# A two-layer hybrid block on one core: K's copies under V's products, the gate's steps spread over the attention, three waits for all engines taken out

## What is computed

```python
h = rmsnorm(x, norm_mix_pre)
q, k, v, rw, gate_a, gate_b = split(h @ w_in)
y_att = sliding_window_attention(rope(q), rope(k), v, sinks) @ w_o_att   # 16 heads, 4 KV heads, window 128
y_rw = rwkv7_time_mix(rw, ...) @ w_o_rw                                  # 16 heads of 64, recurrence over time
mixed = sigmoid(gate_a) * y_att + sigmoid(gate_b) * y_rw
x = x + rmsnorm(mixed @ w_out, norm_mix_post)
```

## Time and profile before

| | |
|---|---|
| time, median of 3 runs (lowest, highest) | 4639.51 us (4636.82, 4644.62) |
| the profiled execution's own time | 4639.49 us |
| its span | 4638.0 us |
| mean granted clock of TensorE | 0.964 |
| busy: TensorE, its weight loads, VectorE, ScalarE, GpSimd | 93%, 73%, 43%, 33%, 12% |
| chain of work that ended last: TensorE | 52% of the span |
| attention of the first layer, first scores to the first column of the output projection | 125.5 to 234.7 us |
| its recurrence (scan), start and end | 489.2 to 664 us |

### The profile page before, as it was taken

The page is one execution under the profiler, slowest core; times in us unless marked ns, Lnnn a source line. Parts: engine busy times, 40 slices in busy tenths (PEclk is TensorE's granted clock), DMA queues, the critical chain, the costliest instruction groups (busy, mean ns, idle before and its releaser), DMA issues.

```text
span 4638.0 us, 76648 instructions
## 1 busy us (share of the span) xinstructions
PE 4333.9 (93%) x33564; PEld 3399.0 (73%) x33564; DVE 1980.6 (43%) x2957; ACT 1528.6 (33%) x2699; POOL 571.7 (12%) x398
## 2 busy tenths in 40 slices
PE   7899999899998899899899998988899999899999
PEld 5676896677776676896677776765778888666877
DVE  4536434455434536434455434347432221443332
ACT  2533232333332533232333333237321121343221
POOL 1215100011002215101011001102000000150000
PEclk9999999999998999999999998999999999899999
DMA  4122101244422122101344421110011111101222
GB/s 147 42 96 72 35 4 60 96 150 167 155 82 101 42 100 73 35 4 60 105 150 164 156 85 41 51 37 1 32 51 64 63 60 60 54 10 55 96 88 90
DMA packets 97647, 351.90 MB, mean 76 GB/s; under 512 B 10017, under 2 KB 13601, under 8 KB 95905
## 3 DMA queue, kind: packets, MB, share of 16 engines
q1 hardware_dynamic: 86432, 313.02, 19.7%
q10 hardware_dynamic: 10880, 33.96, 2.0%
HBM read 332.26 MB, written 14.68 MB: 75 GB/s over the span
## 4 chain that ended last, share of the span: by engine, by line
PE 52%; DVE 4%; ACT 1%; POOL 1%; issue 1%; ACTq 0%; DVEq 0%
PE ps L341 13%; PE ps L342 13%; PE ps L344 13%; PE ps L1260 5%; PE ps L2233 1%; DVE sml L2308 1%; POOL e L2753 1%; PE ps L2668 1%; PE ps L2670 1%; DVE hm_lo L428 1%; PE ps L2669 1%; DVE hm L437 1%; PE ps L2255 1%; PE ps L2536 1%; PE ps L2122 1%
## 5 line engine op out<-in xcount | busy, mean ns | idle before, releaser
L302 DVE TENSOR_TENSOR wlo<-ring,whi 128x1024 fp32r<-128x1024 f32 x494 | 626.2, 1268 | 1911.4 <-ACT whi L292 1911.2
L292 ACT CAST whi<-ring 128x1024 fp32r<-128x1024 f32 x494 | 517.8, 1048 | 2210.8 <-PE ps L344 1916.6
L341 PE MATMUL ps<-h_hi,whi 128*128 128x512 f32 x1424 | 597.6, 420 | 33.1 <-DVE wlo L302 16.5
L342 PE MATMUL ps<-h_lo,whi 128*128 128x512 f32 x1424 | 568.9, 400 | 0.0
L344 PE MATMUL ps<-h_hi,wlo 128*128 128x512 f32 x1424 | 568.1, 399 | 0.0
L341 PE MATMUL ps<-hm_hi,whi 128*128 128x512 f32 (+1 forms) x1408 | 518.6, 368 | 21.3 <-DVE hm_lo L428 21.3
L342 PE MATMUL ps<-hm_lo,whi 128*128 128x512 f32 (+1 forms) x1408 | 483.3, 358 | 0.0
L344 PE MATMUL ps<-hm_hi,wlo 128*128 128x512 f32 (+1 forms) x1408 | 421.3, 357 | 0.0
L341 PEld LDWEIGHTS ps<-h_hi,whi 128*128 128x128 f32 x1424 | 272.6, 191 | 178.8 <-issue 73.0
L341 PEld LDWEIGHTS ps<-hm_hi,whi 128*128 128x128 f32 x1408 | 268.2, 190 | 98.0 <-issue 19.9
L341 PE MATMUL ps<-ac_hi,whi 128*128 128x512 f32 x880 | 330.8, 376 | 6.4 <-DVE ac L2448 6.4
(11 more groups left out here) (394 smaller groups left out, 7610.5 us busy)
## 6 DMA issues: line engine op xcount, KB each, us to landing
ring<-in_w SPq DMA_DIRECT2D x590, 512.0 KB, 3.4
h_spill<-h ACTq DMA_DIRECT2D x2, 2048.0 KB, 6.7
x_spill<-x ACTq DMA_DIRECT2D x2, 2048.0 KB, 14.9
m_spill<-m ACTq DMA_DIRECT2D x2, 2048.0 KB, 9.4
h_again<-h_spill ACTq DMA_DIRECT2D x2, 2048.0 KB, 8.0
ma<-m_spill ACTq DMA_DIRECT2D x2, 2048.0 KB, 10.0
x<-x_spill ACTq DMA_DIRECT2D x2, 2048.0 KB, 10.1
x<-in_x SPq DMA_DIRECT2D x1, 2048.0 KB, 10.8
```

Of the source, the lines that this page charges most:

```text
L292: self.A.copy(self.hi[k % 2][:], raw).then_inc(self.s_cut_hi.h, 1)
L302: self.V.tensor_tensor(self.lo[k % 2][:], raw, self.hi[k % 2][:].bitcast(F32), ALU.subtract).then_inc(self.s_cut_lo.h, 1)
L341: T.matmul(ps[:, b, 0:cw], hi, xh(q, c0, cw), start=q == 0, stop=False, skip_group_check=True)
L342: T.matmul(ps[:, b, 0:cw], hi, xl(q, c0, cw), start=False, stop=False, skip_group_check=True)
```

## The change

Five things change, in both layers of the first block:

1. K's copies: `double(0)` runs before V's first look-ahead cut on ScalarE, `double(1)` after it; V's copy comes before the second cut.
2. The gate's 64 steps are dealt out by a table, `share`: none in round 0, then 4, 6, 3 in each of 14 rounds, 6, 6. `done(it)` gives the columns that end in round `it`. On ScalarE the copy of such a column stands right behind the round's exponentials, and its cuts at the round's end; on VectorE the cuts come before `att_lo`.
3. At the fence after the attention TensorE doesn't wait for the others; it waits for the last tile of `m`.
4. Both fences between the operands and the scan are gone. TensorE waits before each group's first product (`ready(g)`) for what that group reads. The scan's tiles that lie over the operands' last buffers get rooms of their own, and VectorE clears `st` when the last column is done.
5. `recurrence_operands` no longer cuts beyond its own pieces (`hold`). The two cuts left over and the transfer of `h_again` come in the scan, at the thirteenth place of ScalarE's and VectorE's woven programs.

```diff
     def fence(self, T_waits=True):
...
-        self.T.wait_ge(self.s_fence.h, end)
+        if T_waits:
+            self.T.wait_ge(self.s_fence.h, end)
...
-        self.fence()
+        T.wait_ge(self.s_gy.h, self.s_gy.n)
+        self.fence(T_waits=False)
...
-        self.recurrence_operands(hh, hl)
-        self.fence()
-        A.dma_start(self.view("h_again", TMP + 6144, DT, S)[:], self.h_spill.ap()).then_inc(self.s_ld_h.h, 16)
-        self.s_ld_h.take(16)
-        self.recurrence()
+        self.recurrence(*self.recurrence_operands(hh, hl))
...
         def act():
-            for st in rows:
-                if st.at + st.n == PIECE:
-                    self.act_cuts(self.ahead(st.cut))
-            A.wait_ge(self.s_roped.h, b_roped + n_out)
-            for g in range(4):
...
+            ends = [st for st in rows if st.at + st.n == PIECE]
+            double(0)
+            self.act_cuts(self.ahead(ends[0].cut))
+            double(1)
             A.wait_ge(self.s_mm.h, rows[-1].value)
             A.copy(vt[:], ps[:, 0:4, 0:256]).then_inc(self.s_vt.h, 1)
+            self.act_cuts(self.ahead(ends[1].cut))
...
+        share = [0, 4, 6, *[3] * (N - 2), 6, 6]
+        upto = [sum(share[:it + 1]) for it in range(N + 3)]
+
+        def done(it):
+
+            return range((upto[it] - share[it]) // DT, upto[it] // DT)
...
+        def pe_gate(it):
+            for i in range(upto[it] - share[it], upto[it]):
+                j, q = divmod(i, DT)
+                if q == 0 and j >= 1:
+                    T.wait_ge(self.s_gate.h, b_gate + j)
...
                     A.activation(es, es, ACT.Exp).then_inc(self.s_ex.h, 1)
+                act_gate(it)
...
-                    act_gate(j)
+                for j in done(it):
+                    self.act_cuts(self.ahead(cols[j][-1].cut))
...
+        def ready(g):
+
+            T.wait_ge(self.s_pc.h, b_pc + GP * (g + 1))
+            T.wait_ge(self.s_shift.h, b_sh + shifted((2, GP * (g + 1) - 1)) + 1)
+            T.wait_ge(self.s_zb.h, b_zb + N)
+            T.wait_ge(self.s_knn.h, b_knn + DT)
+            if g == 1:
+                T.wait_ge(self.s_bonv.h, b_bonv + DT)
+        return ready, cols[-1][-1].value
...
+        self.V.wait_ge(self.s_mm.h, columns_done)
         self.V.memset(m["st"][:], 0.0)
-        self.fence()
...
+        go(self.and_then(self.woven(lambda g: self.scan_act(g, m, ops, base[g])), 12, self.act_ahead))
+        go(self.and_then(self.woven(lambda g: self.scan_dve(g, m, base[g])), 12, lambda: self.dve_cuts(self.held)))
```

More of the change, by code:

```diff
@@ L534, in act @@
                     if st.at + st.n == PIECE:
-                        self.act_cuts(self.ahead(st.cut))
+                        self.act_cuts(self.ahead(st.cut) if hold is None else min(hold, self.ahead(st.cut)))
                 if act_tick:
@@ L544, in dve @@
                     if st.at + st.n == PIECE:
-                        self.dve_cuts(self.ahead(st.cut))
+                        self.dve_cuts(self.ahead(st.cut) if hold is None else min(hold, self.ahead(st.cut)))
                 if dve_tick:
@@ L817, in pe_values @@
             m.then_inc(self.s_pv.h, 1)
[L819 to L825, removed]
+        def pe_gate(it):
[3 more added lines that the diff above has]
+                    T.wait_ge(self.s_gate.h, b_gate + j)
+                hi, lo = self.halves_of(cols[j][q])
                 T.matmul(ps[:, 7, :], hi, hh(q, 0, S), start=q == 0, stop=False, skip_group_check=True)
@@ L844, in pe, with act_gate @@
             yield
[L846 to L848 removed]
+        def act_gate(it):
+            for j in done(it):
                 A.wait_ge(self.s_mm.h, cols[j][-1].value)
                 A.copy(GA[:, j, :], ps[:, 7, :]).then_inc(self.s_gate.h, 1)
[L851 to L856, removed]
         def dve_low(g):
@@ L933, in dve @@
                     V.tensor_copy(PT[j % 2][:, 0:2, 0:kw], heads(2)[:, :, 0:kw]).then_inc(self.s_ptv.h, 1)
[L934 to L937, removed]
+                for j in done(it):
+                    self.dve_cuts(self.ahead(cols[j][-1].cut))
+                if it >= 3 and steps[it - 3][0] == 3:
+                    dve_low(steps[it - 3][1])
             yield
@@ L1187, in free @@
                 T.wait_ge(self.s_zb.h, b_zb + n - 2)
-        go(*self.dense(cols, hh, hl, SEG1, lambda n: [n % 3], free, None, pe_tick, act_tick, dve_tick, pool_tick))
+        self.held = cols[-1][-1].cut + 2
+        go(*self.dense(cols, hh, hl, SEG1, lambda n: [n % 3], free, None, pe_tick, act_tick, dve_tick, pool_tick,
+                       hold=cols[-1][-1].cut))
         for n in range(N, max(at_bonus) + 1):
@@ L1225, in recurrence, with act_ahead, and_then @@
         base = [(pe[g], act[g], dve[g], pool[g]) for g in range(2)]
-        go(self.woven(lambda g: self.scan_pe(g, m, ops, base[g])))
-        go(self.woven(lambda g: self.scan_act(g, m, ops, base[g])))
-        go(self.woven(lambda g: self.scan_dve(g, m, base[g])))
+        go(self.woven(lambda g: self.scan_pe(g, m, ops, base[g], ready)))
+        go(self.and_then(self.woven(lambda g: self.scan_act(g, m, ops, base[g])), 12, self.act_ahead))
+        go(self.and_then(self.woven(lambda g: self.scan_dve(g, m, base[g])), 12, lambda: self.dve_cuts(self.held)))
         go(self.woven(lambda g: self.scan_pool(g, m, base[g])))
+    def act_ahead(self):
+        A = self.A
+        A.dma_start(self.view("h_again", TMP + 6144, DT, S)[:], self.h_spill.ap()).then_inc(self.s_ld_h.h, 16)
+        self.s_ld_h.take(16)
+        self.act_cuts(self.held)
+    def and_then(self, program, at, f):
+        for i, _ in enumerate(program):
+            if i == at:
+                f()
+            yield
     def woven(self, program):
@@ L1278, in scan_pe @@
         sp = self.s_sp[g].h
+        ready(g)
         for c in range(NCH + 1):
```

31 lines of the change are left out of this document (17 added, 14 removed).

## The result

| | before | after |
|---|---|---|
| time, median (lowest, highest) | 4641.5 us (4636.8, 4645.3), 6 runs | 4659.5 us (4655.8, 4661.4), 6 runs |
| ratio to before, 95% interval | | 1.0036 (1.0025 to 1.0048) |
| span of the profiled execution | 4638.0 us | 4657.0 us |
| mean granted clock | 0.964 | 0.966 |

The change is slower by 17 us (12 to 22). The forecast was +25, so the change in time was forecast 8 too high; the time itself lies 5 us under the forecast time, since the median of the kernel before is 2 us higher over all runs than over the three that the forecast started from.

The account below looks back on a forecast made before the run. TensorE, busy 93% of the span, was taken as the bound. Per layer, attention +13.3 and operands-to-scan -0.8, doubled, gave +25.0 on 4639.5: 4664.5 us; own range 4655 to 4675, 8-in-10 range 4643 to 4683.

Parts of the forecast that it names:

- V's and K's copies: Before the attention's first scores: K's copies run under V's products, only V's copy stays exposed, 6.2 us earlier per layer.
- The waits: Attention, per layer: TensorE's waits, mostly for the gate's copy, sum to 30.1 us against 11.4 before.
- VectorE enters round 6 some 1.8 late: Attention, rounds 7 and 15: round 4's cut delays VectorE 1.8 us, raising the wait from 7.4 to 9.2, twice.
- The clock: Attention, per layer: slow products after five long waits, 1.6 us each, cost 8.0 us, against 7.2 lost before.
- The attention as a whole: Per layer: new waits and clock loss, less the old ones and the 6.2 us from earlier copies, +13.3 us.
- The fence after the attention: End of attention: TensorE leaves once the last gated tile is written, but the fence passes right behind it: 0, at most -0.2.
- Operands to recurrence: Between operands and scan: the scan's first mask can start earlier without the fences and look-ahead subtraction, -3.3 us per layer.
- The held cuts: In the scan: two casts and a subtraction hold VectorE before the second group's `pf`, +2.5 us per layer, bounds 0 and 4.3.
- B: Rival: waits come as worked out, but cost no clock and the held cuts are hidden; 4643.5 us, chance 0.12.
- C: Rival: the gate's copy is in time after all, attention waits stay near those before; 4625.5 us, chance 0.08.
- D: Rival: the scan starts warm, its early product fills the wait and its start runs at full clock; 4642.9 us, chance 0.08.
- E: Rival: long attention waits cost 5.1 us of clock each, 17 in place of 8 in sum; 4682.5 us, chance 0.14.

Follow-up runs that it names:

- the fastest kernel above: Changed kernel with the gate's copy ahead of the round's exponentials on ScalarE and VectorE's low parts done one round later: 4600.4 us, 0.9916.
- Copy first: Changed kernel with one line moved: on ScalarE the gate column's copy stands ahead of the round's exponentials, not behind them: 4615.9 us, 0.9946.
- the last experiment: Copy first kernel with the last two weight cuts done among the operand columns again, not held for the scan; fences stay away: 4622.4 us, 0.9957.

## Why the prediction was right, and where its terms were off

**Direction and mechanism: right; that the time came so near is in part luck.** The loss is the gate's copy behind the exponentials of its own round: 33 us by the table, about 42 back by moving this one copy. But the sum said +12.5 per layer, 25.0 in all, and the layers gave 7.6 and 7.0, 14.6 in all. The other 4.4 of the 19.0 between the two profiled executions lie outside what was changed. With the layers' 14.6 alone the time would have been 4654.1, just under the forecast's own range of 4655 to 4675.

**V's and K's copies, -6.2: right.** First scores -5.3, and 0.9 of lateness before them makes -6.2. Alone they gave -11.6 for two layers.

**The waits, 30.1: 28.6 measured.** Round by round, forecast and trace: round 2 3.2 and 4.6; round 7 9.2 and 7.4; round 10 4.4 and 4.9; round 12 2.7 and 2.8; round 15 9.2 and 7.4; round 17 0.8 and 0.7. In round 12 the cause is the one I gave, VectorE's cut and `att_lo` in a row, but the last to be ready was ScalarE's `pt` and not the weighed `p`. Of rounds 7 and 15 the step that failed is "VectorE enters round 6 some 1.8 late": the mask of round 6 starts 0.6 behind the end of its scores (154.13 against 153.53), and TensorE comes 0.5 later to its wait than the 6.4 I gave it. The 1.8 was taken from a round before the change, one with the cut directly behind it; now the cut of round 4 is two rounds back. For round 2 I had taken 0.6 off for slow scores and let the third exponentials start 9.8 after the first scores; they start 10.5 after them.

**The clock, +0.8 over before: +0.5.** The difference was right and both sides were too high. The attention's products take 91.9 at 1.00 (the fastest kernel above), 97.8 before, 98.4 after: the low level cost 5.9 and 6.5 us where I had 7.2 and 8.0. (Copy first, also at 1.00, takes 93.0 for the same products; by that they are 4.8 and 5.4.) In the changed kernel the low level follows four waits and not the five I counted: 133.4 to 138.0 ran at 0.63, 167.8 to 171.5 at 0.50, 188.8 to 192.5 at 0.57 and 226.5 to 230.3 at 0.60, while the 6 us behind the wait of 2.8 ran at 1.00. Worked out from their busy times, an estimate, these four lost about 1.6 each, which is the price I had used. The Trainium skill (TensorE: Matmul & The Clock Gate, Terms) puts the penalty at half of the throttled time; as an estimate that is 0.08 x 126.9 = 10.2 for the changed kernel. The windows do not agree: about a third of that fell into TensorE's own waits.

**The attention as a whole, +13.3: +11.5** (17.2 more idle, 0.5 more busy, less 6.2).

**The fence after the attention, 0: right.** The wait is 3.1 as in the earlier trace rows, now put down to `m`.

**Operands to recurrence, -3.3: about -4.1 to -4.6.** Bonus product to mask is 1.15 now (497.95 to 499.10) against 3.63 in the earlier trace rows; 1.0 is the shorter tail: GpSimd's product, 2.24 beside the subtraction, takes 1.26 without it; and TensorE waits 0.7 less for `kk_sq` among the operands (7.0 for 7.7). The same code gave less in other kernels: behind the last `m` the first mask came 4.1 earlier in the change and with the fences alone, but 2.6 with the copy first and 1.2 with the low parts later on top. For the product beside the subtraction I had 0.8 and the trace gives 1.0; the 1.1 by the Trainium skill (SBUF — State Buffer, SBUF: two separate sides), an exclusive lock, is as near, so this case cannot tell them apart.

**The held cuts, +2.5: too much for the changed kernel, not elsewhere.** They do stop TensorE, for 1.6 in one stretch. From the first mask to the convolution the changed kernel loses only 0.7, but the fences alone lose 2.3, and holding the cuts costs 2.9 there by the last experiment. The same experiment shows what the sum left too small: the cuts held bring the mask 3.1 earlier, and I had 0.8 for that. Why the changed kernel loses so little in the scan stays open. Forecast for the place -0.8 per layer, measured about -3.9 in the first (and -7.4 for two layers with the fences alone); with the attention's 1.8 this is the whole distance of 5 us in the first layer.

**The rivals.** B's premise (the clock pays nothing for the waits) did not come true: it paid some 6 us a layer. Nor did C's: the copy was never in time. D: the first product of the scan came early, but TensorE then waited 4.3 for the mask and the first 12.2 us of the scan ran at 0.59. E: the waits of 7.4 cost 1.5 to 1.8 each, about what those of 4.6 and 4.9 cost, and not 5.1.

## What to carry to other kernels

Before work is shared out evenly over a software pipeline, look where the thing that releases the next share stands in the other engine's program: a 0.6 us copy behind work that waits for this round made TensorE wait 7.4 us. Each engine here works its program in the order written (ScalarE stood idle for 4.2 us while the copy could have been made), and leftovers (here the low halves) belong behind the next instruction that another engine waits for and not in front of it, above all when the leftover itself waits for another engine. One moved line and one moved block, found from two idle rows (4.21 on ScalarE, 3.23 on VectorE), turned +17 us into -39 us.

## What the runs showed of the hardware that I had not expected

Equal waiting does not cost equal clock. Copy first (13.6 us idle, none longer than 3.2) kept the granted clock at 1.00 and 93.0 us of busy time; copy first with columns that end with a round (13.2 us idle, up to 4.3 at a time) had 0.94 and 97.1. And with the low parts later on the changed kernel the idle time fell by 9 us while the clock fell too, from 0.92 to 0.89, and busy time rose by 2.6. So the clock's price does not follow from the sum of the waits. What it follows from these runs don't tell.
